# adaLN vector-matrix products moved to four column groups of the TensorE array

## The chip, the cores and the metric

The kernel runs on one core of one Trainium2 chip. The metric is the device time of one execution in microseconds; lower is better. Of a kernel that was run several times the median counts.

## The reference, cut to what matters

A first block (gated linear attention and MoBA attention, then a PEER feed-forward over 16384 experts) is followed by a second block of two layers (attention and MLP, then convolution and MLP) on 256 tokens of width 1024. The second block is modulated by adaLN: two vectors, `c` and `c_ctx`, go through SiLU and are multiplied in fp32 with one 1024 x 6144 matrix per layer.

```python
c_act = jax.nn.silu(c)            # 1 x 1024
cc_act = jax.nn.silu(c_ctx)       # 1024
for l in range(2):
    mod = (c_act @ ada_w[l] + ada_b[l])[:, None, :]
    sh1, sc1, g1, sh2, sc2, g2 = jnp.split(mod, 6, axis=-1)
    ...
    mod_c = cc_act @ ada_w[l] + ada_b[l]      # layer 0: the context is modulated too
```

These products are 2 x 1024 times 1024 x 12288, some 50 MB of weights for two rows of result. Nothing else in the two blocks depends on them until the second block begins.

## The kernel before, in words

Each engine has one instruction list in a fixed order; semaphores tie them together. The big projections run as three fp32r products per weight chunk (lines 429 to 433).

The adaLN work is cut into 24 "rows" of 512 output columns. A row k needs four DMA tiles of 512 KB (128 partitions x 1024 floats), each of which serves two of its eight products. `ada_product` (line 490) multiplies chunk c: the stationary operand is `sc[:, 2c:2c+2]` (128 x 2, the SiLU of both vectors), the moving one 128 x 512 of weights, and the result adds up in two partitions of one PSUM bank, `row[0:2, :]`. ACT copies the two partitions to `ada_row` in SBUF (`ada_copy`, line 930). Four transposes per row (`ada_columns`, line 482) turn it into 128 x 8 in another bank, and DVE adds the bias and stores it (`adaln`, line 1298). The columns of row k-1 come ahead of the first product of row k.

The rows are spread by hand over three stages in which TensorE would otherwise wait for softmax or routing work on other engines:

- Stage 1 (rows 0 to 5): rows 0, 1, 2 around the norms and the rotation of MoBA (lines 608 to 614), rows 3 to 5 in pieces of 2 to 4 products in the loop over the eight heads (`ADA_MOBA`, lines 100 and 647 to 657). In that loop each unit is: scores of head n, adaLN products, transposes of head n-2, values of head n-3.
- Stage 2 (rows 6 to 13): the loop that builds the expert gates (lines 691 to 710). Eight turns of eight groups g; each group has one adaLN product and then four 128x128x128 products of one-hot matrices (line 708). The one-hots come from DVE (line 1570) and are scaled on POOL (line 1233); DVE multiplies the result into the expert table (line 1585). Here the weights are loaded from ACT's queue into `ada_x`.
- Stage 3 (rows 14 to 23): rows 14, 15 around the norm and rotation of the second attention (lines 780 to 784), rows 16 to 21 whole in the units of the first softmax loop (`ADA_A`, line 101), rows 22 and 23 in the second one (`ADA_B`, line 102): twice a pair of products, and twelve units with one product.

In stages 1 and 3 SP loads the tiles into a ring of four slots (`load_ada`, line 346). The load of tile n waits until the first product of tile n-3 is done (`ada_started`, raised by every even product). So the last tile of a row is asked for only once the first product of that same row is through. The transposes of a row wait for ACT's copy (`ada_row_ready`) and for DVE's work on the row before (`ada_cols_ready`).

Of the kernel before, what the change touches and what calls it, by code (L numbers as in the profile page):

```python
# [16 lines left out]
P = 128  # L17
# [3 lines left out]
KC = D // P  # L21
# [16 lines left out]
ROUND = 8  # L38
ADA_RING = 4
ADA_BATCH = 4  # L40
NBANK = 4

ALU = mybir.AluOpType
ACT = mybir.ActivationFunctionType
# [6 lines left out]
def columns(*sized):  # L51

    at, where = 0, {}
    for name, n in sized:
# [7 lines left out]
                    ("conv_w", 3 * KC), ("conv_b", KC), ("ln_g", 4 * KC), ("ln_b", 4 * KC), ("lam", 4))  # L62

CON, NCON = columns(("ident", P), ("mean_d", P), ("mean_128", P), ("mean_64", P), ("zeros", P), ("iota", P), ("eps", 1), ("eps_small", 1),
                    ("one", 1))
CON1, NCON1 = columns(("rot", P), ("cos", T), ("sin", T), ("scan", 2 * T), ("gla_mask", 4 * P), ("causal", 3 * P))
CON2, NCON2 = columns(("rot", P), ("cos", T), ("sin", T))

# [14 lines left out]
def softmax_order(n, tag_s, tag_t, per, beside={}):  # L83
# [35 lines left out]
    moba_rope_ready sm1_max sm1_exp sm1_p moba_o_full sq2_ready route_done gate_exp gate_ready eq_i one_j  # L119
    gated_i silu_c mod_ready v_full gated_hi gated_lo lam_in attn_v_full attn_v_ready b_sq b_norm b_rope  # L120
    sm2_max sm2_p attn_oa_full attn_ob_full oa_ready oa_sq res_ready ln_centered ln_sq ln_scaled xm_pool
    x_ready ln_done hid_sq hid_ready mlp_full conv_u_ready out_copied""".split()


def rows(name):
    a, n = VEC[name]
    return slice(a, a + n)


def build(nc, ins, out):  # L130
    with ExitStack() as ctx:
# [3 lines left out]
        def sb(name, n, dt=F32, at=None):  # L135
            if at is None:
                at = place[0]
                place[0] += (4 * n + 31) // 32 * 32
            return nc.alloc_sbuf_tensor_at(name, [P, n], dt, offset=at), at

        raw, _ = sb("raw", RAW * D)
        w_hi, _ = sb("w_hi", UNITS * HALF, F32R)
        w_lo, _ = sb("w_lo", UNITS * HALF, F32R)
        x_hi, x_at = sb("x_hi", KC * T, F32R)
        x_lo, _ = sb("x_lo", KC * T, F32R)
        ada_x, _ = sb("ada_x", 2 * KC * T, F32, x_at)
        vec, _ = sb("vec", NVEC)
        con, _ = sb("con", NCON)
        x_sb, _ = sb("x_sb", KC * T)
        route, _ = sb("route", ADA_RING * D + 512 + 32)  # L150
        small, _ = sb("small", 3072)
        arena, at = sb("arena", NKEYS * T)
        tail = NKEYS * T - (2 * KC * T + 2 * 4 * T)
        tail_r, _ = sb("tail_r", NKEYS * T - tail, F32R, at + 4 * tail)
        bank = [ctx.enter_context(nc.psum_tensor(f"bank{i}", [P, 512], F32)) for i in range(NBANK)]
        acc = [ctx.enter_context(nc.psum_tensor(f"acc{i}", [P, 512], F32)) for i in range(4)]
        s = {name: ctx.enter_context(nc.semaphore(name)) for name in SEMS}
# [9 lines left out]
        def C(name):  # L167
            return con[:, CON[name][0]:CON[name][0] + CON[name][1]]
# [73 lines left out]
        cut3 = carver(small)  # L242
# [5 lines left out]
        smx = cut3(64)  # L248
        mod = cut3(2 * 2 * N_MOD * KC)
        mod1 = cut3(2 * 2 * N_MOD * KC)  # L250
        sc = cut3(2 * KC)
        ln_x = cut3(2 * 3 * KC)
        ln_m = cut3(2 * 3 * KC)
        top = cut3(PEER_H * TOPK)
# [6 lines left out]
        ada_row = cut4(512)  # L261
# [151 lines left out]
        def _(pe):  # L413
            mm = nc.tensor.matmul
# [67 lines left out]
            def ada_columns(k, cols, waited=False):  # L482

                if not waited:
                    wait_row(k)
                for m in range(ADA_BATCH):
                    last = nc.tensor.transpose(cols[:, 2 * m:2 * m + 2], ada_row[0:2, m * P:(m + 1) * P], C("ident")[0:2, 0:2])
                last.then_inc(s["ada_cols_full"], 1)

            def ada_product(row, c, w):  # L490
                return mm(row[0:2, :], sc[:, 2 * c:2 * c + 2], w, start=(c == 0), stop=(c == KC - 1))  # L491

            def ada(k, row, cols, c0=0, c1=KC, first=False):

# [45 lines left out]
            for p in range(2):  # L540
                last = mm(ps[:, p * T:(p + 1) * T], aw[0:GLA_R, p * P:(p + 1) * P], grT[0:GLA_R, :],
                          start=True, stop=True)
# [8 lines left out]
            for tt in range(TT):  # L551
                for p in range(2):
                    a = (tt * 2 + p) * P
                    last = nc.tensor.transpose(ps[:, a:a + P], k_st[:, p * T + tt * P:p * T + (tt + 1) * P], C("ident"))
            last.then_inc(full("kst"), 1)

            for hh in range(2):
                ps = opened("at", hh)
                r = slice(64 * hh, 64 * hh + 64)
                for p in range(2):  # L560
                    for tt in range(TT):
                        cols = slice(p * T + tt * P, p * T + (tt + 1) * P)
                        last = mm(ps[:, cols], k_in[r, cols], q_d[r, cols], start=True, stop=True)
# [5 lines left out]
            for k, chunks in enumerate(((0, 2), (1,))):  # L569
                ps = opened("upd", k)  # L570
                for m, c in enumerate(chunks):
                    r = slice(64 * (c % 2), 64 * (c % 2) + 64)
                    for p in range(2):
                        for hh in range(2):
                            a = (c // 2 * 2 + p) * P + 64 * hh
                            hd = 2 * p + hh
                            last = mm(ps[64 * hh:64 * hh + 64, (m * 2 + p) * P:(m * 2 + p + 1) * P], kst[r, a:a + 64],
                                      gv[r, (c // 2) * 512 + hd * P:(c // 2) * 512 + (hd + 1) * P], start=True, stop=True)
# [6 lines left out]
            for hh in range(2):  # L585
                r = slice(64 * hh, 64 * hh + 64)
                for p in range(2):
                    hd = 2 * p + hh
                    for tt in range(TT):
                        cols = slice(p * T + tt * P, p * T + (tt + 1) * P)  # L590
                        last = mm(acc[hh][:, cols], gv[:, tt * 512 + hd * P:tt * 512 + (hd + 1) * P],
                                  at_sb[:, hh * 512 + p * T + tt * P:hh * 512 + p * T + (tt + 1) * P],
                                  start=True, stop=False, skip_group_check=True)
                        for c in (2 * tt, 2 * tt + 1):
                            if c:
                                a = ((c - 1) * 2 + p) * P
# [66 lines left out]
            for k in range(8):  # L663
# [5 lines left out]
                for m in range(4):  # L669
                    hp = half * 8 + g * 4 + m  # L670
                    a = hp * T + tt * P
# [222 lines left out]
        def _(act):  # L894
            steps = [0]

            def fn(dst, src, f, **kw):
                return nc.scalar.activation(dst, src, f, **kw)  # L898
# [31 lines left out]
            def ada_copy(k, row, i=0):  # L930

                act.wait_ge(s["ada_row_full"], i + (k + 1))
                fn(ada_row[0:2, :], row[0:2, :], ACT.Copy).then_inc(s["ada_row_ready"], 1)

            eps = C("eps")

# [16 lines left out]
            wait_full(act, "ms1")  # L953
            fn(rstd, B("ms1")[:, 0:T], ACT.Sqrt, bias=eps).then_inc(free("ms1"), 1)
            act.wait_ge(s["in_vec"], 16)
            fn(sc, vec[:, rows("c")], ACT.Silu).then_inc(s["silu_c"], 1)
            for half in range(2):
                x_high("xn1", xn, x_hi, half)

# [264 lines left out]

        @block.gpsimd
        def _(pool):
            nc.gpsimd.memset(at_sb, 0.0).then_inc(s["at_zeroed"], 1)

            with pool.Fori(0, 8) as i:
                for g in range(8):  # L1230
                    pool.wait_ge(s["eq_i"], i * 8 + (g + 1))
                    e = ione[:, (g % 2) * 512:(g % 2 + 1) * 512].rearrange("p (t k) -> p t k", t=4)
                    nc.gpsimd.tensor_tensor(e, e, gT[:, bass.ds(i * 32 + 4 * g, 4)].unsqueeze(2).to_broadcast([P, 4, P]),  # L1233
                                            ALU.mult).then_inc(s["gated_i"], 1)

            pool.wait_ge(s["v_full"], 7)
            pool.dma_start(ctx_sb, ins["ctx"]).then_inc(s["in_ctx"], 16)

            for n in range(3):
                pool.wait_ge(s["ln_scaled"], 4 * n + 4)  # L1240
                for c in LN_POOL:
                    last = nc.gpsimd.tensor_scalar(xm[:, c * T:(c + 1) * T], res[:, c * T:(c + 1) * T],
                                                   *ln_factor(ln_m, n, c), ALU.mult, ALU.add)
                last.then_inc(s["xm_pool"], 1)
                for c in range(KC):
                    last = nc.gpsimd.tensor_scalar(x3d[:, c, :], res[:, c * T:(c + 1) * T], *ln_factor(ln_x, n, c),
                                                   ALU.mult, ALU.add)
                last.then_inc(s["x_ready"], 1)
# [692 lines left out]
def constants():  # L1941

    f = np.float32
    q, t = np.arange(P), np.arange(T)

    def rotation(half):

        m = np.zeros((P, P), f)
        first = (q // half) % 2 == 0
        m[q[first] + half, q[first]] = -1.0  # L1950
        m[q[~first] - half, q[~first]] = 1.0
        return m

    def tables(n, angle_of):
        inv = np.power(f(THETA), -np.arange(n, dtype=f) / f(n)).astype(f)
        ang = (angle_of[:, :].astype(f) * inv[q % n][:, None]).astype(f)
        return np.cos(ang).astype(f), np.sin(ang).astype(f)

    con = {"ident": np.eye(P), "mean_d": np.full((P, P), 1.0 / D), "mean_128": np.full((P, P), 1.0 / P),
           "mean_64": (q[:, None] // 64 == q[None, :] // 64) / 64.0, "zeros": np.zeros((P, P)),  # L1960
           "iota": np.tile(q, (P, 1)), "eps": np.full((P, 1), EPS), "eps_small": np.full((P, 1), EPS / 1024.0),
           "one": np.ones((P, 1))}
    cos, sin = tables(HD // 2, np.tile(t, (P, 1)))
    same = (q[:, None] // CHUNK == q[None, :] // CHUNK) & (q[:, None] <= q[None, :])
    causal = np.where(np.concatenate([q[None, :], t[None, :]], 1) <= np.concatenate(
        [np.tile(q[:, None], (1, P)), np.tile(q[:, None] + P, (1, T))], 1), 0.0, -1e30)
    con1 = {"rot": rotation(HD // 2), "cos": cos, "sin": sin,
            "scan": np.tile((np.arange(2 * T) % CHUNK != 0).astype(f), (P, 1)),
            "gla_mask": np.tile(same.astype(f), (1, 4)), "causal": causal}

    by_row = (q % HD < HD // 2)[:, None]
    cos2, sin2 = tables(HD // 4, np.where(by_row, t[None, :] // 64, t[None, :] % 64))
    con2 = {"rot": rotation(HD // 4), "cos": cos2, "sin": sin2}
    return {"con": np.concatenate([con[n] for n in CON], 1), "con1": np.concatenate([con1[n] for n in CON1], 1),
            "con2": np.concatenate([con2[n] for n in CON2], 1)}
# [13 lines left out]
```

## Time and profile before

| | us |
|---|---|
| median of 3 runs | 2041.83 (2040.65 to 2043.28) |
| profiled execution, span | 2040.7 |
| TensorE matmul busy | 1905.0 (93%) |
| VectorE busy | 1302.6 (64%) |
| ScalarE busy | 838.8 (41%) |
| GpSimd busy | 112.2 (5%) |

The profiled execution is one run; its span goes from the first to the last instruction of the core, and the median of the shown runs is 1.1 us above it. The page gives busy time by engine, the chain of work that ended last, and groups of instructions by source line. Of TensorE the matmuls (PE) and the weight loads (PEld) are told apart. An fp32 matmul shows as two instructions, each with its weight load. The time of one instruction contains the passage through the array, so instructions that follow each other overlap in the records; the distance from start to start is what each costs in a stream. The timeline merges neighbours of one line and gives start, duration, engine, line, operands, count, and in brackets the idle time before it with what ended it.

### The profile page before, as it was taken

Reading aid. Unit: us, or ns where it says so; the run is one execution under the profiler, and the core shown is the slowest. Engines: PE = TensorE matmul, PEld = TensorE weight load, DVE = VectorE, ACT = ScalarE, POOL = GpSimd, SP = SyncE. Lnnn points to the kernel's source line nnn. Section 1 sums busy time; section 2 is a strip of 40 time slices with the busy share of each in tenths; the row PEclk is TensorE's granted clock in tenths of the full one; section 3 lists DMA queues with packets and bytes.
Section 4 is the critical chain, followed back from the end, with each engine's and each line's share of the span. In section 5 each row is a group of like instructions: output and inputs, shape, how many; then the busy total and the mean of one; then the engine's idle time right before and its main releaser. Section 6 shows DMA issues by size and latency. Waiting matters only on the chain.

```text
span 2040.7 us, 38045 instructions
## 1 busy us (share of the span) xinstructions
PE 1905.0 (93%) x13780; PEld 1674.4 (82%) x13780; DVE 1302.6 (64%) x2467; ACT 838.8 (41%) x1517; POOL 112.2 (5%) x100
## 2 busy tenths in 40 slices
PE   6989899999999888999999979898989997989997
PEld 5934899999999444899999979434679997979997
DVE  4475558878744999655655562535766666666665
ACT  5423454455454000455555543122334443434443
POOL 0000000000000555000000000000010001010000
PEclk9999999999999999999999989999999998989999
DMA  6444445555556332455655553262135553625552
GB/s 247 135 132 137 136 155 180 180 177 183 178 179 188 123 103 92 135 184 182 200 183 185 180 185 106 75 209 97 63 112 183 178 185 105 185 90 177 180 185 78
DMA packets 86349, 314.71 MB, mean 154 GB/s; under 512 B 9600, under 2 KB 9744, under 8 KB 85904
## 3 DMA queue, kind: packets, MB, share of 16 engines
q1 hardware_dynamic: 80208, 292.06, 44.7%
q10 hardware_dynamic: 5936, 20.79, 3.1%
q0 software_dynamic: 144, 1.05, 0.1%
q8 instruction: 38, 0.62, 0.1%
q14 instruction: 23, 0.19, 0.0%
HBM read 312.82 MB, written 1.05 MB: 154 GB/s over the span
## 4 chain that ended last, share of the span: by engine, by line
PE 83%; DVE 8%; issue 5%; ACT 1%; DMA 1%; POOL 1%; DVEq 0%; ACTq 0%; POOLq 0%; SPq 0%
PE bank L431 14%; PE bank L432 14%; PE bank L433 14%; PE acc L431 10%; PE acc L432 10%; PE acc L433 10%; PE acc L491 4%; DVE route L1570 3%; PE bank L513 2%; PE acc L807 1%; PE bank L521 1%; PE bank L790 1%; DVE arena L1372 1%; PE bank L708 1%; PE bank L799 1%
## 5 line engine op out<-in xcount | busy, mean ns | idle before, releaser
L1273 DVE TENSOR_TENSOR w_lo<-raw,w_hi 128x512 fp32r<-128x512 f32 x982 | 652.6, 689 | 473.1 <-ACT w_hi L898 472.1
L898 ACT ACTIVATE w_hi<-raw 128x512 fp32r<-128x512 f32 x982 | 594.1, 628 | 419.1 <-PE acc L431 268.5
L431 PE MATMUL bank<-x_hi,w_hi 128*128 128x256 f32 x2224 | 639.0, 287 | 55.5 <-DVE x_lo L1282 24.5
L432 PE MATMUL bank<-x_lo,w_hi 128*128 128x256 f32 x2224 | 635.8, 286 | 0.0
L433 PE MATMUL bank<-x_hi,w_lo 128*128 128x256 f32 x2224 | 635.6, 286 | 0.0
L431 PEld LDWEIGHTS bank<-x_hi,w_hi 128*128 128x128 f32 x2224 | 433.8, 195 | 61.3 <-issue 39.0
L432 PEld LDWEIGHTS bank<-x_lo,w_hi 128*128 128x128 f32 x2224 | 434.0, 195 | 0.0
L433 PEld LDWEIGHTS bank<-x_hi,w_lo 128*128 128x128 f32 x2224 | 433.6, 195 | 0.0
L431 PE MATMUL acc<-x_hi,w_hi 128*128 128x256 f32 x1024 | 290.2, 283 | 0.0
L432 PE MATMUL acc<-x_lo,w_hi 128*128 128x256 f32 x1024 | 289.8, 283 | 0.0
L433 PE MATMUL acc<-x_hi,w_lo 128*128 128x256 f32 x1024 | 289.8, 283 | 0.0
L898 ACT ACTIVATE arena<-bank 128x256 f32<-128x256 f32 (+3 forms) x164 | 84.1, 513 | 319.0 <-PE bank L433 311.3
L432 PEld LDWEIGHTS acc<-x_lo,w_hi 128*128 128x128 f32 x1024 | 196.6, 192 | 0.2 <-issue 0.2
L431 PEld LDWEIGHTS acc<-x_hi,w_hi 128*128 128x128 f32 x1024 | 196.6, 192 | 0.2 <-issue 0.2
L433 PEld LDWEIGHTS acc<-x_hi,w_lo 128*128 128x128 f32 x1024 | 196.6, 192 | 0.0
L431 PE MATMUL acc<-tail_r,w_hi 128*128 128x256 f32 x512 | 144.1, 281 | 0.0
L432 PE MATMUL acc<-tail_r,w_hi 128*128 128x256 f32 x512 | 144.1, 281 | 0.0
L433 PE MATMUL acc<-tail_r,w_lo 128*128 128x256 f32 x512 | 144.0, 281 | 0.0
L708 PEld LDWEIGHTS bank<-route 128*128 128x128 f32 x512 | 63.0, 194 | 78.2 <-issue 78.2
L1233 POOL TENSOR_TENSOR route<-route 128x512 f32<-128x512 f32 x64 | 84.1, 1314 | 734.8 <-DVE route L1570 734.8
L491 PE MATMUL acc<-route,small 128*2 128x512 f32 x256 | 118.3, 604 | 4.1 <-DVE arena L1723 3.2
L898 ACT ACTIVATE route<-acc 2x512 f32<-2x512 f32 x24 | 14.0, 584 | 233.3 <-PE acc L491 233.3
(219 smaller groups left out, 2032.8 us busy)
## 6 DMA issues: line engine op xcount, KB each, us to landing
raw<-in_peer_u SPq DMA_DIRECT2D x128, 512.0 KB, 3.3
raw<-in_peer_v SPq DMA_DIRECT2D x128, 512.0 KB, 3.3
raw<-in_mlp_w SPq DMA_DIRECT2D x128, 512.0 KB, 3.4
route<-in_ada_w SPq DMA_DIRECT2D x64, 512.0 KB, 4.3
ada_x<-in_ada_w ACTq DMA_DIRECT2D x32, 512.0 KB, 3.3
raw<-in_w_in SPq DMA_DIRECT2D x25, 512.0 KB, 3.8
raw<-in_conv_w_in SPq DMA_DIRECT2D x24, 512.0 KB, 3.9
raw<-in_attn_w_in SPq DMA_DIRECT2D x18, 512.0 KB, 3.5
```

The costliest lines, as they stand in the source:

```text
L431: first = mm(dst, a[0], b[0], start=start, stop=False, **kw)
L432: mm(dst, a[0], b[1], start=False, stop=False, **kw)
L433: return first, mm(dst, a[1], b[0], start=False, stop=stop, **kw)
L491: return mm(row[0:2, :], sc[:, 2 * c:2 * c + 2], w, start=(c == 0), stop=(c == KC - 1))
L513: last = mm(ps[:, 0:T], C("mean_d"), src[:, c, :], start=(c == 0), stop=(c == KC - 1))
L521: mm(ps[:, 0:n], weights, src[:, 512 * k:512 * k + n], start=True, stop=True)\
L708: last = mm(ps[:, t * P:(t + 1) * P], jone[:, a:a + P], ione[:, a:a + P], start=True, stop=True)
L790: mm(ps[:, 0:T], lhsT, qk[r, k_ctx * T:(k_ctx + 1) * T], start=True, stop=True)
L898: return nc.scalar.activation(dst, src, f, **kw)
L1233: nc.gpsimd.tensor_tensor(e, e, gT[:, bass.ds(i * 32 + 4 * g, 4)].unsqueeze(2).to_broadcast([P, 4, P]), ALU.mult).then_inc(s["gated_i"], 1)
L1273: v.tensor_tensor(w_lo[:, unit(n, half)], raw[:, a:a + HALF], w_hi[:, unit(n, half)].bitcast(F32), ALU.subtract).then_inc(s["lo_done"], 1)
L1570: v.tensor_tensor(dst[:, half * 512:(half + 1) * 512].rearrange("p (t k) -> p t k", t=4), C("iota").unsqueeze(1).to_broadcast(shape), inde ...
```

## The change

- `sc` becomes 128 x (32 x 8): 32 columns per chunk, of which two hold the values and 30 are zero. POOL zeroes it at the start, and the SiLU writes the two live columns of each chunk after a wait on the new semaphore `sc_zeroed`.
- Product c writes 32 partitions, `row[a:a+32, :]` with a = 32 (c mod 4). So chunks 0 and 4 add up in partitions 0 to 31, 1 and 5 in 32 to 63, and so on. Before, all eight added up in partitions 0 and 1.
- `ada_copy` copies 128 partitions x 512 in place of 2 x 512.
- `ada_columns` multiplies each 128 x 128 block of `ada_row` (stationary, fp32) with a 128 x 2 matrix `sum_groups`, which is 1 where partition mod 32 equals the column, in place of a transpose of 2 x 128 by the identity. Count and place of these four operations per row stay.
- The order of all work, the loads and their waits stay as they were.

```diff
+ADA_COLS = 32
-                    ("one", 1))
+                    ("one", 1), ("sum_groups", 2))
-        small, _ = sb("small", 3072)
+        small, _ = sb("small", 3328)
-        sc = cut3(2 * KC)
+        sc = cut3(ADA_COLS * KC)
                 for m in range(ADA_BATCH):
-                    last = nc.tensor.transpose(cols[:, 2 * m:2 * m + 2], ada_row[0:2, m * P:(m + 1) * P], C("ident")[0:2, 0:2])
+                    last = mm(cols[:, 2 * m:2 * m + 2], ada_row[:, m * P:(m + 1) * P], C("sum_groups"), start=True, stop=True)
             def ada_product(row, c, w):
-                return mm(row[0:2, :], sc[:, 2 * c:2 * c + 2], w, start=(c == 0), stop=(c == KC - 1))
+                a = c % 4 * ADA_COLS
+                return mm(row[a:a + ADA_COLS, :], sc[:, c * ADA_COLS:(c + 1) * ADA_COLS], w, start=(c < 4), stop=(c >= 4))
                 act.wait_ge(s["ada_row_full"], i + (k + 1))
-                fn(ada_row[0:2, :], row[0:2, :], ACT.Copy).then_inc(s["ada_row_ready"], 1)
+                fn(ada_row[:, :], row[:, :], ACT.Copy).then_inc(s["ada_row_ready"], 1)
             act.wait_ge(s["in_vec"], 16)
-            fn(sc, vec[:, rows("c")], ACT.Silu).then_inc(s["silu_c"], 1)
+            act.wait_ge(s["sc_zeroed"], 1)
+            fn(sc.rearrange("p (c v) -> p c v", v=ADA_COLS)[:, :, 0:2], vec[:, rows("c")].rearrange("p (c v) -> p c v", v=2),
+               ACT.Silu).then_inc(s["silu_c"], 1)
         def _(pool):
+            nc.gpsimd.memset(sc, 0.0).then_inc(s["sc_zeroed"], 1)
             nc.gpsimd.memset(at_sb, 0.0).then_inc(s["at_zeroed"], 1)
+           "one": np.ones((P, 1)), "sum_groups": (q[:, None] % ADA_COLS == np.arange(2)[None, :])}
```

## Rows read from the trace of the kernel before

**Rows 1.** The page: busy by engine, and one group.

```profile
PE 1905.0 (93%) x13780; PEld 1674.4 (82%) x13780; DVE 1302.6 (64%) x2467; ACT 838.8 (41%) x1517; POOL 112.2 (5%) x100
...
L491 PE MATMUL acc<-route,small 128*2 128x512 f32 x256 | 118.3, 604 | 4.1 <-DVE arena L1723 3.2
```

**Rows 2.** Timeline of TensorE in stage 1: start, duration, engine, line, operands, count.

```profile
117.93 7.03 PE L491 MATMUL acc<-route,small 128*2 128x512 f32 x16
...
143.19 9.82 PE L491 MATMUL acc<-route,small 128*2 128x512 f32 x16
```

**Rows 3.** Timeline of DVE in stage 1, ahead of the heads.

```profile
117.14 12.95 DVE L1372 RECIPROCAL arena<-arena 128x2048 f32<-128x2048 f32 x1 [5.39 <-ACT arena L898]
...
142.40 0.16 DVE L1302 TENSOR_TENSOR small<-acc,vec 128x8 f32<-128x8 f32 x1
...
147.51 2.29 DVE L1407 TENSOR_TENSOR arena<-arena 128x2048 f32<-128x2048 f32 x1
```

**Rows 4.** Timeline of TensorE in the loop over the heads.

```profile
152.94 0.48 PE L621 MATMUL bank<-arena 64*128 64x128 f32 x2
...
168.56 0.48 PE L621 MATMUL bank<-arena 64*128 64x128 f32 x2
...
169.41 2.74 PE L491 MATMUL acc<-route,small 128*2 128x512 f32 x6
...
173.35 0.49 PE L621 MATMUL bank<-arena 64*128 64x128 f32 x2
...
192.17 0.40 PE L487 MATMUL acc<-con,route 2*128 2x2 f32 x4
```

**Rows 5.** Timeline of DVE in the unit that begins at 168.56.

```profile
169.52 0.56 DVE L1422 SCALAR_TENSOR_TENSOR arena<-bank,arena 128x384 f32<-128x384 f32 x1 [2.52 <-PE bank L622]
...
170.84 0.55 DVE L1416 COPY arena<-bank 128x384 f32<-128x384 f32 x1
```

**Rows 6.** Line 577: timeline, then one window (busy and instructions in flight by engine).

```profile
77.36 1.15 PE L577 MATMUL bank<-arena 64*64 64x128 f32 x24
...
78.16:78.18 0.02, 0.02 (x12) 0.02 (x4) 1.00 0.99 410
```

**Rows 7.** Timeline of TensorE at line 742, weights 128x128, two columns streamed.

```profile
1195.47 0.31 PEld L742 LDWEIGHTS bank<-route,con 128*128 128x128 f32 x2
```

**Rows 8.** Timeline of stage 2 where one turn of eight groups ends.

```profile
704.63 1.13 PE L708 MATMUL bank<-route 128*128 128x128 f32 x8 [0.32 <-POOL route L1233]
...
705.69 0.41 PE L487 MATMUL acc<-con,route 2*128 2x2 f32 x4
...
705.92 1.28 DVE L1585 TENSOR_TENSOR arena<-bank,arena 128x512 f32 x1
...
706.03 1.02 PE L491 MATMUL acc<-ada_x,small 128*2 128x512 f32 x2
707.04 1.13 PE L708 MATMUL bank<-route 128*128 128x128 f32 x8
...
708.42 1.30 DVE L1585 TENSOR_TENSOR arena<-bank,arena 128x512 f32 x1
```

**Rows 9.** Timeline of TensorE in stage 3, rows 17 and 19.

```profile
1343.23 1.88 PE L491 MATMUL acc<-route,small 128*2 128x512 f32 x4 [0.95 <-DMA route<-in_ada_w]
...
1359.79 7.03 PE L491 MATMUL acc<-route,small 128*2 128x512 f32 x16
```

**Rows 10.** Windows there: length, busy PE, PEld, DVE, ACT, POOL, clock, DMA, GB/s.

```profile
1360.00:1362.00 2.00, 2.00 (x6) 0.41 (x5) 1.90 (x7) 0.93 (x3) 0.00 (x0) 1.00 0.04 6
1362.00:1364.00 2.00, 2.00 (x6) 0.36 (x5) 1.25 (x3) 0.52 (x2) 0.00 (x0) 1.00 0.87 264
```

**Rows 11.** Clock: one window as above, then timeline rows of stage 3.

```profile
190.00:200.00 10.00, 7.86 (x48) 6.72 (x47) 5.42 (x12) 3.35 (x5) 0.00 (x0) 0.83 0.14 42
...
1310.17 8.83 PE L521 MATMUL bank<-arena 128*128 128x512 f32 x14 [5.69 <-DVE arena L1649]
...
1403.35 1.88 PE L491 MATMUL acc<-route,small 128*2 128x512 f32 x4 [3.17 <-DVE arena L1723]
```

More of the change, by code:

```diff
@@ L121 @@
     sm2_max sm2_p attn_oa_full attn_ob_full oa_ready oa_sq res_ready ln_centered ln_sq ln_scaled xm_pool
-    x_ready ln_done hid_sq hid_ready mlp_full conv_u_ready out_copied""".split()
+    x_ready ln_done sc_zeroed hid_sq hid_ready mlp_full conv_u_ready out_copied""".split()
 def rows(name):
@@ L1961, in constants @@
            "iota": np.tile(q, (P, 1)), "eps": np.full((P, 1), EPS), "eps_small": np.full((P, 1), EPS / 1024.0),
-           "one": np.ones((P, 1))}
+           "one": np.ones((P, 1)), "sum_groups": (q[:, None] % ADA_COLS == np.arange(2)[None, :])}
     cos, sin = tables(HD // 2, np.tile(t, (P, 1)))
```

## The prediction, made before the changed kernel was run

> **What bounds the kernel now.** I read the page first: TensorE is busy 93% of the span [rows 1], so a shorter product can count. Next I read line 491 by itself. Each fp32 product is two instructions. Sixteen of them (one row) last 7.03 us, one of them 0.60, so they start (7.03 - 0.60)/15 = 0.43 apart and a product costs 0.86 in a stream [rows 1, 2]. With 24 rows of eight that is 192 x 0.86 = 165 us, 8% of the span. The share says little by itself, since the products were put where TensorE waits for others. So I went through the three stages by timeline and asked of each which wait ends last.
>
> Ahead of the heads (117 to 152 us) it is DVE: its reciprocal lasts until 130.1, it reaches the adaLN step at 142.4, and the rotated q and k are ready at 147.51 + 2.29 = 149.8 [rows 3]. TensorE's rows 0 and 1 lie under that. Row 2 starts at 143.19, takes 9.82 and not 7.03, since the clock was down, and ends at 152.9, where the first scores start [rows 2, 4]. In the loop over heads (152.94 to 192.17, 39.2 us) TensorE is the bound: a unit from 168.56 to 173.35 is 4.79 long, DVE idled 2.52 before it [rows 4, 5]. In stage 2 DVE is the bound: it works without a gap (its multiplies at 705.92 and 708.42 have only its own other work between them, 2.5 us with the adaLN step), while TensorE idled 0.32 before a group, though not behind the transposes that end a turn [rows 8]. In rows 16 to 21 of stage 3 TensorE is the bound with the loads close behind: it even waited 0.95 for a tile [rows 9].
>
> **Do column groups overlap?** The trace of before has no four column groups. The nearest row is line 577: 64x64 tiles that alternate between two halves of the columns, first with the upper and then with the lower half of the rows. 24 instructions of 128 columns take 1.15 us with 0.27 for the last, so they start 0.88/23 = 0.038 apart, where one alone would need a quarter of 0.43, 0.107. At 78.16 twelve are in flight [rows 6]. At the beginning two start together, by the windows, though the second instruction of the first product stands between them in the program. So neighbours in other column groups do run beside each other, and four tiles at once by the end. I take four groups: up to four products in 0.86, about 0.9 with the change of mode. Bounds: two at a time, or none.
>
> The Trainium skill (TensorE: Matmul & The Clock Gate, Part 3, The mechanism) says of matmuls that they are "strict FIFO, no reordering". As each product is two instructions to one group, by that rule only the second of one and the first of the next would overlap; the windows at line 577 speak against it. What it would make of the time is the second rival.
>
> **What each part costs.**
> 1. Columns of a row, 24 times. Four transposes step 706.03 - 705.69 = 0.34 [rows 8]. The new products have full 128x128 weights and are two instructions each. The nearest row is line 742: two such loads take 0.31, the last 0.19, so 0.12 apart [rows 7]. 8 x 0.12 = 0.96, that is +0.62 a row where nothing hides it. Bounds: 8 x 0.085 = 0.68 (the transposes' own step) and 1.3.
> 2. ACT's copy of 128 partitions and the weight load of 32 columns: a copy's time goes by its 512 columns, and the load lies under 0.43 of streaming. The memset of 256 columns on POOL and the wait for it are over long before the SiLU, and `sc` is not needed until 117.9. Nothing for these, but 0 to 0.05 per product.
> 3. Stage 1, ahead of the heads. Rows 0 and 1 get shorter under DVE's reciprocal: no gain. Row 2 starts at 142.7 as before, since its columns wait for DVE. Its last tile is asked for when its first product is done. With the columns and a first product at low clock that is about 146, and the tile comes 3.2 later (below), so the row ends near 151: gain 1.9, of 3.1 that the scores could gain at most.
> 4. Stage 1, heads. After the scores (0.85) a unit has three products (2.67, now about 0.9), transposes 0.48 and values 0.79. By the sum TensorE would need 3.02. But the values wait for DVE's copy: scores end 0.92 after the unit begins, DVE starts at 0.96, the copy ends at 170.84 + 0.55 = 2.83, and the values add 0.79 and 0.1 of signal [rows 4, 5]. So 3.72 is the new bound, 3.98 where a row's columns stand in the unit. I ran the eight units with these: starts at 0, 2.7, 4.5, 6.7, 10.7, 14.4, 18.1, 22.1, and the loop's last three units end at 29.2, against 39.2 now: gain 10.0. After the idle time TensorE enters with its clock down: as in rows 2 (9.82 for 7.03) that costs about 2.5. Stage 1 in all: 1.9 + 10.0 - 2.5 = 9.4 gained. What follows is bound by TensorE and moves forward with it. The columns at 192.17 lie under a wait for DVE.
> 5. Stage 2. A single product stands between full-array ones: nothing overlaps. Behind the columns, +0.62 moves the products at 707.04 to 707.66 and their end to 708.79. DVE, which would start at 708.42 and never waits, starts 0.06 behind that: +0.43 in each of seven turns, 3.0 lost. Bounds 1 and 5.
> 6. Stage 3. Rows 14 and 15 lie under DVE's reciprocal and rotation: no gain. Row 16 to 21: the products would need 1.7 in place of 6.9, but the row's last tile sets the end. In row 19 its first product is done at 1360.8; until 1362 hardly any byte moves, then 264 GB/s, so the 524 kB land near 1364, 3.2 after the signal [rows 9, 10]. A row is then 1.0 + 3.2 to 4.2 (the next tile is now asked for at nearly the same moment) + 0.9 = 5.1 to 6.1, gain 0.9 to 1.8, less 0.62 for columns: 0.7 net, 4.0 for six. TensorE idles ahead of the first unit (clock down, 2.0 lost): 2.0 gained. Two pairs in the second softmax loop gain 0.86 each, one row of columns costs 0.62, twelve single products 0.4 together [rows 11, 2]: 0.7 gained.
>
> **Sum.** -9.4 + 3.0 - 2.0 - 0.7 = -9.1. Against the span of 2040.7 that is 2031.6, and with the 1.1 between span and median 2032.7.
>
> **The rivals.**
> - Two at a time. Three products need 4 steps of 0.43, four need 5, a pair 3. In the heads' units this adds 0.86, 0.86, 0.43, 0.86, 0.16, 0, 1.3, 0.6 = 5.1, and 0.9 in the pairs. Rows 16 to 21 stay, as the loads set them. -9.1 + 6.0 = -3.1: 2038.7. For it: no fp32 stream of four groups is in the trace; against it: rows 6.
> - The clock takes it back. In rows 16 to 21 TensorE would now wait some 2.5 us in each row for the last tile. A wait of 2.1 us at 194 stands in a window of clock 0.83; after 5.69 idle the rotation ran at half clock; yet after 3.17 idle a pair took 1.88, full speed [rows 11]. If it falls in every unit, some 3.4 of the other work runs at half speed, +1.7 for each of six: -9.1 + 10 = +1: 2042.
> - More than I take: the clock stays up at both entries (+4.5) and the last tile comes in 3.2 (+3): -16.6: 2025.
> - Slower: the change does not do what it says and the products do not overlap. Then every row stays as it is and the columns cost 0.62 wherever TensorE is the bound: three rows in the heads, six in the first softmax loop, one in the second, 6.2, and 3.0 in stage 2: +9.2: 2051. It decides from the point where a group must end before the next starts; four streams of 128 partitions might get in each other's way. Rows 6 speak against it for two streams.
>
> **How the numbers follow.** Forecast 0.50, two at a time 0.14, the clock 0.14, more 0.12, no overlap 0.10. The predicted time is the forecast's, 2032.7. Its own range, from the bounds of the columns, the loads and the entry clock, is 2027 to 2038. The range for 8 in 10 reaches from the "more" case to the clock's: 2022 to 2043. A measurement of this kernel tells some 0.2% (4 us) from nothing. Faster by more: 0.9 of the forecast, a third of two at a time, some of the clock's, all of "more": 0.67. Within: 0.21. Slower: no overlap and the worse part of the clock case: 0.12.
>
> **What would show it.** A whole row of eight products with its tiles there (row 0) takes about 2.2 us in place of 7.03. Units of the heads step 3.7 to 4.0, DVE nearly without idle time. Columns step 0.96. In stage 2 DVE waits about 0.4 once per turn and the stage grows by 3. Rows 16 to 21 show a wait for the DMA in every row, of 2 to 3 us. Wrong I would be by a row 0 of 3.9 us (two at a time) or 6.9, by half clock in the softmax loops, or by loads that come later once they are asked for closer together.

## The result and the profile after

The changed kernel takes 2051.33 us (median of 20 runs, 2043.59 to 2055.75) where the kernel before takes 2041.41 (20 runs on the same chip, 2036.29 to 2045.75): 1.0043 times as long, 95% interval 1.0034 to 1.0052. The forecast was 9.1 us faster; it became 9.9 slower, outside the range of 2022 to 2043. The profiled execution has a span of 2050.8, against 2040.7.

Line numbers moved: the product is line 493 now (was 491), the columns 488 (487), the scores of a head 623 (621), the gates' products 710 (708), DVE's multiply in the gates 1590 (1585).

The page of after, the lines that answer to [rows 1]: busy by engine, the granted clock in 40 slices of 51 us, and the chain that ended last.

```profile
PE 1890.2 (92%) x13876; PEld 1694.9 (83%) x13876; DVE 1303.5 (64%) x2467; ACT 839.5 (41%) x1517; POOL 112.5 (5%) x101
...
PEclk9977999999999999999999999879999999989999
...
PE 82%; DVE 9%; issue 5%; DMA 2%; ACT 1%; POOL 0%; DVEq 0%; ACTq 0%; POOLq 0%; SPq 0%
```

TensorE is busy 15 us less than before although the span is 10 longer, so the products did get shorter. Two dips stand out in the clock: slices 3 and 4 (103 to 205 us, stage 1) and slices 26 and 27 (1282 to 1384, the first softmax loop). The mean granted clock is 0.956; it was 0.976. Over the 20 runs the time goes with this clock: the shortest, 2043.59, had 0.962 and the longest, 2055.75, had 0.953.

The same points of the program in both timelines, start times in us:

| point | before | after | gained (-) or lost (+) since the point above | forecast |
|---|---|---|---|---|
| last columns of the heads' loop | 192.17 | 192.63 | +0.5 | -9.4 |
| first one-hot product of the gates (stage 2 begins) | 666.8 | 665.7 | -1.6 | 0 |
| end of stage 2 | 823.4 | 824.9 | +2.6 | +3.0 |
| first scores of the second attention | 1327.2 | 1327.4 | -1.3 | 0 |
| columns at the end of the first softmax loop | 1397.74 | 1404.77 | +6.9 | -2.0 |
| last columns, second softmax loop | 1460.95 | 1470.52 | +2.5 | -0.7 |
| end | 2040.7 | 2050.8 | +0.5 | 0 |

Three places carry the error: the heads' loop with what stands ahead of it (9.9 us worse than forecast), the first softmax loop (8.9) and the second (3.2).

**The products overlap, and the heads' loop runs slowly.** TensorE's timeline of after, with the same columns as [rows 2] and [rows 4]:

```profile
118.30 1.92 PE L493 MATMUL acc<-route,small 128*32 128x512 f32 x16
...
144.84 3.63 PE L493 MATMUL acc<-route,small 128*32 128x512 f32 x12
...
150.24 1.05 PE L493 MATMUL acc<-route,small 128*32 128x512 f32 x4 [1.77 <-DMA route<-in_ada_w]
151.22 0.49 PE L623 MATMUL bank<-arena 64*128 64x128 f32 x2
...
192.63 1.05 PE L488 MATMUL acc<-con,route 128*128 128x2 f32 x8
```

Row 0 takes 1.92 us where it took 7.03 [rows 2]: sixteen instructions in the time that four took in one group (1.88, [rows 9]). Row 2 ends and the scores start at 151.2, as forecast (151). But the loop over the heads then lasts from 151.22 to 192.63, 41.4 us, and not 29.2. TensorE by stretches of that loop (width, then busy time and count of PE, PEld, DVE, ACT, POOL, then granted clock, DMA share, GB/s):

```profile
148.00:152.00 4.00, 2.23 (x10) 0.66 (x8) 3.38 (x3) 0.61 (x2) 0.00 (x0) 0.92 0.81 291
152.00:160.00 8.00, 8.00 (x28) 3.93 (x28) 3.46 (x12) 3.23 (x9) 0.00 (x0) 0.51 0.70 227
160.00:170.00 10.00, 9.95 (x32) 4.58 (x31) 4.44 (x16) 2.45 (x9) 0.00 (x0) 0.50 0.36 120
170.00:180.00 10.00, 9.51 (x36) 4.11 (x35) 4.83 (x16) 2.10 (x9) 0.00 (x0) 0.70 0.51 167
180.00:190.00 10.00, 9.04 (x53) 4.46 (x51) 6.13 (x22) 2.92 (x10) 0.00 (x0) 1.00 0.44 149
```

From 152 to about 176 the clock is at its lower level of 1.2 GHz, with TensorE shown busy nearly all the time. It was not low at the first scores: they take 0.49, as in [rows 4], and the granted clock is 1.00 from 149 until 152, the last wait for a tile (1.77) included. It falls 0.8 us behind the first scores. In the kernel before all stretches from 152 to 190 have 1.00, the first of them:

```profile
152.00:160.00 8.00, 8.00 (x27) 2.28 (x25) 3.36 (x12) 3.66 (x10) 0.00 (x0) 1.00 0.77 228
```

**The first softmax loop waits for its tiles.** TensorE's timeline of after, one row with its columns, then the sum of such waits in the view of waits from 1290 to 1410 (idle us, how often, the longest), then one stretch:

```profile
1329.39 1.86 PE L488 MATMUL acc<-con,route 128*128 128x2 f32 x8
1331.18 3.63 PE L493 MATMUL acc<-route,small 128*32 128x512 f32 x12
...
1336.77 1.92 PE L493 MATMUL acc<-route,small 128*32 128x512 f32 x4 [1.96 <-DMA route<-in_ada_w]
```
```profile
PE acc L493 <- DMA route<-in_ada_w: 18.2, 9, 3.0
```
```profile
1350.00:1360.00 10.00, 7.27 (x27) 2.65 (x29) 2.22 (x7) 2.05 (x5) 0.00 (x0) 0.67 0.53 180
```

Six products go through, then the last two wait 2 to 3 us for the row's last tile; that is so in every row (one of the nine waits, 2.77, is row 15's, ahead of the loop). The granted clock is 0.50 from 1330 to 1340; of the stretches of 10 us that follow four stand between 0.67 and 0.84 and two at 0.98 and 1.00. From its first product to the instruction behind its last, rows 16 to 21 take 7.44, 5.82, 7.72, 6.48, 5.89 and 6.65 us, 6.7 in the mean: hardly less than the 7.0 of a row before.

**Stage 2** went as forecast. Both views of one turn, TensorE and DVE:

```profile
704.48 0.95 PE L488 MATMUL acc<-con,route 128*128 128x2 f32 x8
704.80 1.30 DVE L1590 TENSOR_TENSOR arena<-bank,arena 128x512 f32 x1
705.37 1.05 PE L493 MATMUL acc<-ada_x,small 128*32 128x512 f32 x2
...
707.75 1.30 DVE L1590 TENSOR_TENSOR arena<-bank,arena 128x512 f32 x1
```

The columns hold the next product off by 705.37 - 704.48 = 0.89 (0.34 before [rows 8], forecast 0.96), and DVE's multiplies are 707.75 - 704.80 = 2.95 apart where they were 2.50: +0.45, forecast 0.43.

### The profile page after: what moved, and what is told of

Its sections match the earlier page's. It is cut to its first block, busy times and chain, and to the rows that moved or that the text cites. A ratio compares the mean times of both kernels' runs of the same rounds, so it can differ in the third digit from the quotient of the medians.

```text
span 2050.8 us, 38239 instructions
## 1 busy us (share of the span) xinstructions
PE 1890.2 (92%) x13876; PEld 1694.9 (83%) x13876; DVE 1303.5 (64%) x2467; ACT 839.5 (41%) x1517; POOL 112.5 (5%) x101
## 4 chain that ended last, share of the span: by engine, by line
PE 82%; DVE 9%; issue 5%; DMA 2%; ACT 1%; POOL 0%; DVEq 0%; ACTq 0%; POOLq 0%; SPq 0%
PE bank L432 14%; PE bank L434 14%; PE bank L433 14%; PE acc L432 10%; PE acc L434 10%; PE acc L433 10%; DVE route L1575 3%; PE acc L493 2%; PE bank L515 2%; DMA route<-in_ada_w 2%; PE acc L809 1%; PE acc L488 1%; PE bank L792 1%; PE bank L523 1%; PE bank L801 1%
## 5 line engine op out<-in xcount | busy, mean ns | idle before, releaser
L900 ACT ACTIVATE route<-acc 128x512 f32<-128x512 f32 x24 | 14.3, 595 | 231.1 <-PE acc L493 231.1
L432 PEld LDWEIGHTS acc<-tail_r,w_hi 128*128 128x128 f32 x512 | 96.4, 188 | 0.0
```

What stands on the lines that cost most here:

```text
L432: first = mm(dst, a[0], b[0], start=start, stop=False, **kw)
```

## The experiments

Two theories stood at the start. **The program around the products:** they overlap, and the gain is lost since the shorter rows leave TensorE's clock low at the head of the loop over the heads, and since the last tile of a row is asked for only after that row's first product. **The new form itself:** full-array sums, weights of 32 columns or four groups at once slow down what stands beside them or keep the clock low, so that the loss goes with the count of grouped rows.

Eight of the kernels choose per row between the old and the new form. Their common edit, with `grouped(k)` as each entry says (ACT's copy has the same condition):

```diff
+            def grouped(k):
+                return ...
 ...
-                    last = mm(cols[...], ada_row[:, m * P:(m + 1) * P], C("sum_groups"), ...)
+                    if grouped(k): last = mm(cols[...], ada_row[:, m * P:(m + 1) * P], C("sum_groups"), ...)
+                    else: last = nc.tensor.transpose(cols[...], ada_row[0:2, m * P:(m + 1) * P], C("ident")[0:2, 0:2])
 ...
+                if not grouped(k):
+                    return mm(row[0:2, :], sc[:, c * ADA_COLS:c * ADA_COLS + 2], w, start=(c == 0), stop=(c == KC - 1))
 ...
-                fn(ada_row[:, :], row[:, :], ACT.Copy)
+                n = P if grouped(k) else 2
+                fn(ada_row[0:n, :], row[0:n, :], ACT.Copy)
```

An ungrouped row is thus the old one but for the stride in `sc`. Ratios are to the kernel before on the same chip, with 95% intervals. The kernel before had 2042.16 beside the first four kernels, 2041.42 beside the next four and 2042.21 beside the last three.

### Which stage loses

```diff
+                return k < ADA_1                          # s1_only: rows 0 to 5
+                return ADA_1 <= k < ADA_1 + ADA_GATES     # s2_only: rows 6 to 13
+                return k >= ADA_1 + ADA_GATES             # s3_only: rows 14 to 23
```

> Column groups and the summing product only in stage 1 (rows 0 to 5); rows 6 to 23 multiply and transpose as before. The stage-by-stage comparison of the two traces says that stage 1 came out even: the scores begin 1.7 us earlier, but the clock stays at half until 176. Expected if each stage pays by itself: the time of before, within 2 us. If instead the low clock is a thing of the whole program and not of the stage, the heads' loop would run at full clock here and the kernel would be some 8 us faster than before.

Measured: 2041.48 (12 runs), 0.9992 (0.9979 to 1.0005).

> Column groups only in stage 2 (rows 6 to 13), where single products stand between full-array ones. By the step of the columns (0.98 in place of 0.34, seven turns in which DVE then waits): 2 to 3 us slower than before. A rival puts the cost on the change of mode at each of the 64 products: then each group of 2.40 us would be longer and the stage slower by 5 us or more.

Measured: 2045.33 (12 runs), 1.0013 (1.0004 to 1.0021).

> Column groups only in stage 3 (rows 14 to 23). The traces put nearly all of the loss here: 9 us slower than before (range 7 to 11), with a wait for the last tile of each of rows 16 to 21 and the clock at half in between. If the loss came from stage 1's clock instead, this one would be about even.

Measured: 2048.2 (12 runs), 1.0030 (1.0017 to 1.0044).

The ratios stand for -1.6, +2.7 and +6.1 us; their sum, +7.2, is near the +8.8 that the whole change has by its own ratio of 1.0043. Within the intervals the stages add up: stage 3 loses most, though less than the 9 expected, stage 2 loses its 3 us, and in stage 1 the shorter products bring next to nothing. The stretch of low clock in the heads' loop is not of a fixed length: in the trace of `s1_only` it ends at 164 and not at 176, and the loop takes 37.1 us.

### The late tile

```diff
-                    sp.wait_ge(s["ada_started"], i * ADA_RING + (n + 2 - ADA_RING))
+                    if n % ADA_BATCH == ADA_BATCH - 1:
+                        sp.wait_ge(s["ada_row_full"], i + n // ADA_BATCH)
+                    else:
+                        sp.wait_ge(s["ada_started"], i * ADA_RING + (n + 2 - ADA_RING))
```

The last tile of a row is asked for when the row ahead is complete, and no longer after the first product of its own row. The slot has been free since then. `early_tile` is the change with this edit, `before_early` the kernel before with it.

> The changed kernel, but the last tile of each row is asked for when the row before it is complete, and not only after the first product of its own row. Theory 'loads first': the waits of 2 to 3 us in rows 16 to 21 go, the clock then stays up in the softmax units, and the time falls below before, to about 2030. Theory 'clock first': the waits go or shrink (6 x 2.5 = 15 us of waiting), but with less streaming TensorE stays at half clock for much of the units; the time falls only to about 2040 to 2046, and stage 1's heads (152 to 176) stay at half clock though they have no wait for a tile.

Measured: 2033.7 (6 runs), 0.9950 (0.9933 to 0.9967).

> The kernel before, only with the last tile of a row asked for when the row before it is complete. It waited for a tile 0.95 us once and for eleven small ones, so: 1 to 3 us faster than before. If the early request by itself were what made the changed kernel faster, this would reach 2034.

Measured: 2041.87 (11 runs), 1.0001 (0.9992 to 1.0010).

The same edit is worth 17.6 us to the change and nothing to the kernel before (1 to 3 were expected), whose rows of 7 us covered nearly all of the transfer. In the trace of `early_tile`, the sum of the waits from 1290 to 1410, one row, and a stretch of the first softmax loop:

```profile
PE acc L496 <- DMA route<-in_ada_w: 3.5, 10, 1.1
```
```profile
1353.91 1.92 PE L496 MATMUL acc<-route,small 128*32 128x512 f32 x16
```
```profile
1340.00:1350.00 10.00, 8.44 (x49) 3.73 (x48) 4.34 (x11) 2.65 (x6) 0.00 (x0) 1.00 0.90 284
```

The waits shrink from 18.2 to 3.5 us, some rows go through in 1.92 at a stretch, and the clock is 1.00 from 1340 to 1370 (0.79 in the 10 us ahead, 0.93 and 0.84 in the 20 behind). The loop, from first scores (1324.74) to last columns (1383.43), takes 58.7 us in place of 77.4, which is nearly the whole 19.4 between the two profiled spans. Of these 18.7 some 12 are waits inside the loop (14.7 less row 15's 2.77); the rest goes with the clock. The heads' loop is little changed in this kernel (148.70 to 188.86, 40.2 us, at 0.50 from 150 until 173), though no wait for a tile stands ahead of it: TensorE waits 1.99 for DVE there.

### The clock at the entry to the heads

```diff
+                return 3 <= k < 6      # heads_only: rows 0 to 2 ahead of the loop stay as they were
+                return 2 <= k < 6      # row2_too
```

> Column groups only for rows 3 to 5, in the loop over the heads; rows 0 to 2 ahead of it multiply as before, so TensorE streams until the first scores and enters with its clock up. If the half clock from 152 to 176 was brought along from the idle time ahead, the loop of 39.2 us shortens to about 30 (the 10.0 of the prediction), and the kernel to about 2032. If the clock falls inside the loop anyhow, as the units now stream less, the gain is 0 to 4 us.

Measured: 2033.97 (5 runs), 0.9963 (0.9949 to 0.9976).

> As the kernel with column groups for rows 3 to 5, with row 2 in groups as well. Row 2 then streams for some 3.4 us in place of 9.8 just ahead of the first scores. If what counts is the clock with which TensorE enters the heads' loop, this one row should undo most of that kernel's gain: half clock until 165 or 176 as in the changed kernel, time 2037 to 2042 against 2034. If the entry does not matter, the shorter row 2 adds up to 3 us of gain: 2031 to 2034.

Measured: 2040.76 (11 runs), 0.9992 (0.9982 to 1.0002).

One row more in groups, the one right ahead of the loop, costs 6.8 us by the medians and 5.9 by the ratios, most of the gain of 7.6 that `heads_only` has by its own. TensorE's timeline of `heads_only` at the entry, in two full-speed units and at the end, and its stretches:

```profile
142.78 9.95 PE L499 MATMUL acc<-route,small 128*2 128x512 f32 x16
152.66 0.48 PE L631 MATMUL bank<-arena 64*128 64x128 f32 x2
...
168.71 0.48 PE L631 MATMUL bank<-arena 64*128 64x128 f32 x2
...
172.38 0.49 PE L631 MATMUL bank<-arena 64*128 64x128 f32 x2
...
184.54 1.05 PE L492 MATMUL acc<-con,route 128*128 128x2 f32 x8
```
```profile
144.00:152.00 8.00, 8.00 (x14) 1.31 (x13) 6.33 (x5) 0.00 (x0) 0.00 (x0) 0.71 0.50 150
152.00:160.00 8.00, 6.92 (x34) 2.51 (x32) 4.81 (x18) 3.96 (x11) 0.00 (x0) 1.00 0.83 279
160.00:168.00 8.00, 7.51 (x46) 3.79 (x43) 4.88 (x18) 2.90 (x12) 0.00 (x0) 1.00 0.63 215
```

The old row 2 streams for 9.95 us without a break. It begins at half speed, and the loop is entered and gone through at 1.00, even though TensorE is busy only 6.92 to 7.51 of 8 us in it. A unit is 172.38 - 168.71 = 3.67 long (forecast 3.72), the loop 184.54 - 152.66 = 31.9. The same stretches of `row2_too`:

```profile
144.00:152.00 8.00, 5.78 (x20) 1.49 (x12) 6.76 (x6) 0.93 (x2) 0.00 (x0) 0.50 0.57 195
152.00:160.00 8.00, 8.00 (x28) 3.53 (x27) 3.46 (x12) 2.67 (x8) 0.00 (x0) 0.50 0.51 170
160.00:168.00 8.00, 8.00 (x26) 4.08 (x28) 4.34 (x16) 2.70 (x11) 0.00 (x0) 0.50 0.51 161
```

Here row 2 is six products, 2.22 us of wait for its last tile, and two products. The clock stays at 0.50 through it and for some 24 us of the loop, which lasts 41.3 us. The instructions of the loop are the same in both kernels; what differs is what TensorE did in the 10 us ahead of it, an unbroken stream or a short one with a wait of 2 us. The level at the first scores is not the whole of it: in the changed kernel, in `s1_only` and in `early_tile` the clock is 1.00 when they begin, behind waits of 1.77, 2.18 and 1.99 us, and falls within 1.5 us. No kernel has a short row 2 without such a wait, so which of the two counts isn't separated.

### Is it the new form?

```diff
-                a = c % 4 * ADA_COLS
-                return mm(row[a:a + ADA_COLS, :], sc[...], w, start=(c < 4), stop=(c >= 4))
+                return mm(row[0:ADA_COLS, :], sc[...], w, start=(c == 0), stop=(c == KC - 1))
 ...
-                fn(ada_row[:, :], row[:, :], ACT.Copy)
+                fn(ada_row[0:ADA_COLS, :], row[0:ADA_COLS, :], ACT.Copy)
 ...
-            act.wait_ge(s["sc_zeroed"], 1)
+            act.wait_ge(s["sc_zeroed"], 2)
 ...
+            nc.gpsimd.memset(ada_row[:, :], 0.0).then_inc(s["sc_zeroed"], 1)
```

All eight products of a row go to the first group; the padding, the sums and their full weights stay, the overlap is gone.

> The changed kernel with all eight products of a row in column group 0 (32 padded columns, one after the other); the sum over 128 partitions stays, the other three groups' partitions of the row in SBUF are zeroed once. Each product again takes 0.86 us by itself. Theory 'less streaming': the clock stays up in the heads' loop as before, and the kernel pays only the columns, 0.62 where TensorE is the bound: 2041 + 6 + 3, so about 2050. Rival 'narrow or padded streams do not count': the clock stays at half in the heads here too, and the time is well above that, 2060 or more.

Measured: 2052.48 (5 runs), 1.0051 (1.0037 to 1.0064). The heads' stretches of its trace:

```profile
152.00:160.00 8.00, 8.00 (x29) 3.16 (x28) 2.26 (x8) 2.85 (x6) 0.00 (x0) 1.00 0.73 213
160.00:168.00 8.00, 8.00 (x31) 3.25 (x29) 5.13 (x20) 3.19 (x12) 0.00 (x0) 1.00 0.55 192
```

By the ratio it loses 10.4 us, the price of the sums together with the padded weights (my fourth rival had 9.2 for a change without overlap), and its clock is 1.00 in the heads and 0.975 in the mean (0.976 before). So neither the padded weights nor the sums lower the clock. Four groups at once don't either: in `heads_only` the loop has them and stands at 1.00. And the loss doesn't go with the count of grouped rows: three make that kernel faster. In the changed kernel the overlap does bring its time, and other things take it away again: two kernels of nearly the same time with quite different reasons.

### Undoing only the entries

```diff
+                return k not in (0, 1, 2, 14, 15)      # entry_old
```

> The changed kernel, but rows 0, 1, 2, 14 and 15 (the ones that lie under DVE's work ahead of the two softmax stages) multiply and transpose as before. The late request of each row's last tile stays. If the clock on entry is worth what the stages suggest, stage 1 gains 7 and the first units of stage 3 about 2 to 3: 2051 - 10 = 2041 to 2044. If the waits for the last tile are what lowers the clock in stage 3 by themselves, its units still swing between the two clocks here.

Measured: 2040.93 (11 runs), 0.9991 (0.9981 to 1.0001). It is 10.4 us below the change. The heads' loop runs at 1.00 again and its last columns come at 185.03, 7.6 us earlier. The first softmax loop is entered at full clock too, but rows 19 to 21 still wait 2.73, 2.81 and 3.06 us for their last tile, the four stretches of 10 us from 1350 to 1390 stand at 0.79 to 0.85, and the loop takes 73.2 us (77.4 in the change, 70.5 before). So there the waits lower the clock also behind a good entry.

### What is best kept

```diff
+                return 3 <= k < 6 or 16 <= k < 22      # hybrid_late; hybrid_early: with the earlier request too
```

> Column groups for rows 3 to 5 and 16 to 21 only, with the late request of the last tile as in the kernels before and after. Against the same kernel with the early request (2024.2) it shows what that request is worth when entry is at full clock: five to six waits of 2 to 3 us, so 2036 to 2040. Against rows 3 to 5 alone (2034.0) it shows whether rows 16 to 21 gain or lose by groups: the prediction had 2 us of gain, the changed kernel 7 us of loss; expected here a loss of 2 to 6.

Measured: 2036.31 (10 runs), 0.9973 (0.9959 to 0.9986).

> Column groups for rows 3 to 5 and 16 to 21 only, the places where TensorE was the bound and several products stand together; rows 0 to 2, 14, 15, the gates' rows and the single products as before, and the last tile asked for early. Expected: no loss in the gates (3 us) and in the single products (2.5 us), full clock on entry at 152 and 1327: 2033.7 less 5 to 10, so 2024 to 2029. If streaming less lets the clock fall inside the loops, 2029 to 2034.

Measured: 2024.17 (5 runs), 0.9910 (0.9896 to 0.9923).

Groups only where TensorE is the bound and in streams of two products or more, with the last tile asked for earlier, make the kernel 17 us faster than before. The earlier request is worth 12.1 of them. Without it the groups in rows 16 to 21 lose 2.3 us against `heads_only`, as expected. Two rows of the timeline of each, `hybrid_late` first:

```profile
1353.17 1.05 PE L501 MATMUL acc<-route,small 128*32 128x512 f32 x4 [2.85 <-DMA route<-in_ada_w]
...
1374.85 1.68 PE L501 MATMUL acc<-route,small 128*32 128x512 f32 x4 [2.90 <-DMA route<-in_ada_w]
```
```profile
1344.88 1.92 PE L504 MATMUL acc<-route,small 128*32 128x512 f32 x16
...
1353.60 1.05 PE L504 MATMUL acc<-route,small 128*32 128x512 f32 x4 [1.00 <-DMA route<-in_ada_w]
```

In `hybrid_early` the first softmax loop, from first scores to last columns, takes 57.3 us; it took 70.5 before and 77.4 after the change. The loads now come close to bounding it: TensorE still waits for tiles nine times, 5.1 us in all, and the stretch from 1350 to 1360 has the DMA engines at 0.84 and 287 GB/s.

## Why the prediction was wrong

**Do the groups overlap, and the rival of two at a time (2038.7).** The overlap was right, and full: 1.92 us for a row, where two at a time would give about 3.9. The four groups' fp32 streams pass as one. (The prediction calls two at a time the second rival; in its list it is the first, and "the clock takes it back" is the second.) The Trainium skill's "strict FIFO, no reordering" (TensorE: Matmul & The Clock Gate, Part 3, The mechanism), read as a bar to overlap behind a product's second instruction, is contradicted by this row: sixteen instructions last as long as four.

**Step 1, columns.** 0.98 us between the first of a row's columns and its first product in a full-speed row of `hybrid_early`, 0.89 in stage 2; forecast 0.96. Right.

**Step 2, ACT's copy and the padded weights.** ACT is busy 839.5 us for 838.8, and a row goes through in 1.92. Right.

**Step 3, ahead of the heads.** 151.2 for 151. Right in time, but this was the step in which the cause of the next error lay: I counted what the shorter rows 0, 1 and 2 bring (nothing and 1.9) and not what they had done for TensorE's clock.

**Step 4, the heads.** The bound of a unit was right (3.67 for 3.72). What failed is its last term, "that costs about 2.5". I took this from row 2 of before, 9.82 for 7.03, as if coming back to 2.4 GHz had a fixed price. That row was one unbroken stream, and behind it the clock was up. In the loop's own units it stayed at 1.2 GHz until about 176. The loop is 41.4 - 29.2 = 12.2 us longer than the one I added up. With the clock up it is 31.9 (`heads_only`), so the clock's term measures 41.4 - 31.9 = 9.5 in place of 2.5; `row2_too`, one row different, has 41.3. Of the other 2.7, waits for tiles at 159.48 and 179.03 are 1.08 and 0.65 (`heads_only`). Both parts together eat the gain of 10.0.

**Step 5, stage 2.** +0.45 a turn for +0.43, +2.6 for +3.0, and alone +2.7. Right.

**Step 6, the first softmax loop.** That the last tile would set the end, and that TensorE would wait 2 to 3 us for it in each row, came true (1.96 to 3.00). What failed is what the waits do: I let the clock drop only once, at the entry, and put the falling in every unit into the second rival, "the clock takes it back", at 0.14. That rival is what happened here, with nearly its price: it had +10 against the forecast, measured are 8.9. Its total, 2042, lies below the 2051 measured mainly since it left out the heads' loop. `early_tile` shows that the waits carry it: with most of them gone the stretches from 1340 to 1370 stand at 1.00. The length of a row was bounded rightly: rows 17 and 20, mostly at full clock, take 5.8 and 5.9 of my 5.1 to 6.1, while rows 16 and 18, at half clock for most of their length, take 7.4 and 7.7. That I took [rows 11], a pair at full speed after 3.17 idle, as speaking against it was the mistake: in the changed kernel the same wait, again 3.17, was followed by half speed.

```profile
1410.93 1.30 PE L493 MATMUL acc<-route,small 128*32 128x512 f32 x4 [3.17 <-DVE arena L1728]
...
1415.21 1.92 PE L493 MATMUL acc<-route,small 128*32 128x512 f32 x2
```

A single product takes 1.92 here, as long as a full row at the upper level. The form of the products isn't the reason: in `hybrid_early` the pair at this place is in the old form, and behind the same 3.17 it took 3.01 us in place of 1.88.

```profile
1380.04 3.01 PE L502 MATMUL acc<-route,small 128*2 128x512 f32 x4 [3.17 <-DVE arena L1740]
```

So the same idle time goes either way, and one row bears no rule. This is also the likely cause of the second softmax loop's +2.5 for -0.7; no run isolates it.

**The range** was too narrow since the entry clock was given a bound of its own (0 to 2.5) and not the whole length of the loop that follows, and since both large errors are of the clock and came together, where each alone (9.9 and 8.9) would have stayed within it. The time came within 1 us of the case without overlap (2051), by luck: row 0 shows that the products do overlap.

**Slips in the sums.** Six rows of 0.7 are 4.2 and not 4.0, and the clock's case is 2041.8 + 1 = 2042.8 and not 2042. Neither moves the outcome.

**Open.** Why the clock stays at half for some 24 us in which TensorE shows 8.00 of 8.00 busy, and why for only some 14 in `s1_only`. No run isolates it. Streams put in only to keep the clock up weren't tried.

## What to carry to other kernels

Work that TensorE does while it waits for another engine can also keep its clock up for what follows: before shortening it, look at the granted clock in the first microseconds of the next loop bound by TensorE, and price a low one with the whole loop and not with one row. Where a stream gets shorter than the transfer that follows it around a ring of buffers, move the request for the last slot forward with it: here the same edit was worth nothing to the old rows and 12 to 18 us to the new ones. Shorten only where the engine is the bound, and test the overlap apart from the schedule around it, since a total alone (2051 and 2052 here) did not tell a working overlap from none.

## What the hardware showed that was not expected

- Four fp32 streams to four column groups took as long as one: 1.92 us for sixteen instructions of 512 columns (after), against 7.03 in one group, 3.7 times, and 1.88 for four instructions in one group (before).
- The same loop over the heads ran at either level: behind an unbroken stream of 9.95 us at 1.00, with TensorE busy 6.92 to 7.51 of 8 us (`heads_only`), and behind a short row with a wait of 2.22 us at 0.50 for some 24 us, with TensorE shown busy 8.00 of 8 (`row2_too`). The busy share of the profile doesn't tell which.
- In the changed kernel the clock was 1.00 at the first scores and fell 0.8 us later, behind a wait of 1.77 us.
- An idle time of 3.17 us ahead of the same pair of products was followed by 2.4 GHz in one profile (1.88 us, before) and by 1.2 GHz in another (3.01 us, `hybrid_early`).
- With a wait of 2 to 3 us in each row of the first softmax loop the granted clock of its stretches was 0.50 to 0.84 (after); with the waits mostly gone it was 1.00 (`early_tile`, 1340 to 1350).
